# One ring of split weight buffers across four stages of a float32 transformer layer, with expert dots rescheduled and a load moved to another queue

## The reference, cut to what matters

```python
q = (xt @ w_q).reshape(t, PEER_HEADS, 2, PEER_HALF)
sc = jnp.einsum("thpc,hpnc->thpn", q, sub_keys)
top_s, top_i = lax.top_k(sc, PEER_TOPK)
...
best_s, best_pos = lax.top_k(cand_s, PEER_TOPK)
idx = jnp.take_along_axis(cand_i, best_pos, axis=-1)
gate = jax.nn.softmax(best_s, axis=-1)
...
act = jnp.einsum("cd,ced->ce", xc, u[ic])
hid = jax.nn.gelu(act) * gc
return jnp.einsum("ce,ced->cd", hid, v[ic])
```

## Time and profile before

| | |
|---|---|
| median of 3 runs | 2314.18 us (2313.13 to 2315.13) |
| the profiled execution | 2311.03 us, span 2309.1 us |
| TensorE busy | 2165.0 us, 94% of the span |
| TensorE's mean granted clock | 0.968 of 2.4 GHz |
| VectorE, ScalarE, GpSimd busy | 65%, 36%, 29% |
| to 552.5 us | projection, attention, merge, query |
| 552.5 to 1050 us | table |
| 1050 to 1759 us | experts |
| from 1759 us | second layer, output |

### The profile page before, as it was taken

One profiled execution on the slowest core, in us unless ns is written; L12 is line 12 of the kernel. 1 busy time (PEld: TensorE's weight loads), 2 busy tenths in 40 slices (PEclk: granted clock), 3 DMA queues, 4 the chain that ended last, 5 costly groups with the idle time before them and its releaser, 6 DMA issues. The chain is left out here.

```text
span 2309.1 us, 28625 instructions
## 1 busy us (share of the span) xinstructions
PE 2165.0 (94%) x10851; PEld 1874.2 (81%) x10851; DVE 1501.2 (65%) x2669; ACT 826.5 (36%) x1318; POOL 662.4 (29%) x436
## 2 busy tenths in 40 slices
PE   7999899899999978998999999999997999988898
PEld 6777788688999878998788787899986798876677
DVE  4645433325899867864898898869897634447634
ACT  3344423322333324773333333333334332222322
POOL 0100000000117878751444444526661000014200
PEclk9999999999999989999999999999998999988899
DMA  5321533211677766898999999979993322210220
GB/s 209 117 87 47 201 146 124 105 37 51 225 231 211 207 147 149 214 245 292 353 382 388 386 384 375 385 256 381 363 360 122 118 89 95 91 55 1 110 100 37
DMA packets 220089, 454.52 MB, mean 197 GB/s; under 512 B 32305, under 2 KB 137777, under 8 KB 213169
## 3 DMA queue, kind: packets, MB, share of 16 engines
q1 hardware_dynamic: 164656, 318.39, 40.4%
q0 software_dynamic: 55296, 134.31, 17.7%
HBM read 406.17 MB, written 46.47 MB: 196 GB/s over the span
## 5 line engine op out<-in xcount | busy, mean ns | idle before, releaser
L1662 PE MATMUL bank<-Vh,Hh 128*128 128x512 f32 x768 | 302.6, 394 | 14.6 <-DVE Hl L1745 14.6
L1663 PE MATMUL bank<-Vl,Hh 128*128 128x512 f32 x768 | 301.7, 393 | 0.0
L1664 PE MATMUL bank<-Vh,Hl 128*128 128x512 f32 x768 | 301.6, 393 | 0.0
L940 PE MATMUL bank<-XH,Ue 128*128 128x384 f32 x736 | 256.0, 348 | 29.4 <-DVE Ue L929 29.4
L1022 POOL DMA_INDIRECT gates<-rows_sb x128 | 236.4, 1847 | 58.1 <-issue 36.6
L941 PE MATMUL bank<-XL,Ue 128*128 128x384 f32 x736 | 251.4, 342 | 0.0
L942 PE MATMUL bank<-XH,Ue 128*128 128x384 f32 x736 | 251.3, 341 | 0.0
L1684 ACT ACTIVATE Vh<-Vr 128x1024 fp32r<-128x1024 f32 x128 | 135.8, 1061 | 289.0 <-PE bank L1664 181.7
L978 POOL DMA_INDIRECT ring<-in_v,gidx x128 | 187.8, 1467 | 172.2 <-DVE x_res L990 73.6
L978 POOL DMA_INDIRECT ring<-in_u_rows,gidx x98 | 128.8, 1315 | 225.1 <-DVE ghid L983 181.1
L1740 DVE TENSOR_TENSOR Vl<-Vr,Vh 128x1024 fp32r<-128x1024 f32 x128 | 156.3, 1221 | 51.4 <-ACT Vh L1684 51.2
(11 more groups left out here) (394 smaller groups left out, 4845.2 us busy)
## 6 DMA issues: line engine op xcount, KB each, us to landing
Vr<-in_v SPq DMA_DIRECT2D x128, 512.0 KB, 10.1
ur<-in_u SPq DMA_DIRECT2D x86, 512.0 KB, 4.3
W<-in_w_stream SPq DMA_DIRECT2D x19, 2048.0 KB, 8.2
Gr<-gates SPq DMA_DIRECT2D x32, 768.0 KB, 13.9
XT<-in_u SPq DMA_DIRECT2D x42, 512.0 KB, 5.3
early<-ar SPq DMA_DIRECT2D x92, 192.0 KB, 2.3
A<-early SPq DMA_DIRECT2D x92, 192.0 KB, 11.0
xs<-in_w_mixer SPq DMA_DIRECT2D x14, 1024.0 KB, 5.0
```

The source lines that it names most:

```text
L940: pe.matmul(ps, h[:, k], c.Xh[:, k, 0:DN], start=k == 0, stop=False)
L1662: pe.matmul(ps, Hh[r][:, tok], Vh[r][:, cut], start=p == 0, stop=False)
L1663: pe.matmul(ps, Hh[r][:, tok], Vl[r][:, cut], start=False, stop=False)
L1664: mm = pe.matmul(ps, Hl[r][:, tok], Vh[r][:, cut], start=False, stop=p == PK - 1)
```

## The change

The low half of the attention's `kq` tensor now lives from attention to the experts; its upper part holds one ring of two high and two low halves (`c.H`, `c.L`), used by merge, query, table and experts alike. So halves can be made ahead of a border:

- merge piece 0 inside attention, eight units before its end;
- query pieces 0 and 1 inside merge, and query piece 0's product too, behind merge's transposes;
- the table's first two `u` blocks inside query (in place of `hi(16)`, `hi(17)`);
- the experts' first two at the table's end.

The multiplication that makes the fourth tile's input row (`gat.x`) moves from the end of merge into query (after piece 3) and becomes one operation. Blocks per selection and dots per selection change; no fetch is issued between scatter puts. In the experts' stage the gate loads from block 8 on are issued by ScalarE instead of SP, the second gate load comes two steps later, the wait for the stored activations comes after the lead, and `norm_f` is loaded after iteration 8 instead of at the start. Query products use banks 4 to 7 and scores banks 0 to 3.

```diff
-E_SCORE, E_MID, E_SLICES, E_LAST = (14, 19, 19, 19), 0, 8, 5
+E_SCORE, E_MID, E_SLICES, E_LAST = (16, 21, 18, 17), 0, 8, 4
-DOTS = (0, 10, 10, 10)
+DOTS = (0, 12, 4, 0)
...
+    def shared(self, ctx):
+        self.kq = ctx.enter_context(self.nc.sbuf_tensor("kq", [P, LOW + 4 * KT * P], F32))
+        top = self.nc.sbuf_base
+        self.H, self.L = ([self.nc.alloc_sbuf_tensor_at(f"{n}{i}", [P, KT * P], F32R, offset=top - (at - i) * KT * P * 4)[:] for i in range(2)]
+                          for n, at in (("H", 4), ("L", 2)))
...
 # phase_attend, AHEAD = UNITS - 2 * TT
 # VectorE
             for i in range(UNITS + 4):
+                if i == AHEAD + 1:
+                    dve.wait_ge(c.whi, W_MERGE + 1)
+                    dve.tensor_tensor(c.L[0], c.w(B_MERGE, KT * P).rearrange("p k c -> p (k c)"), c.H[0].bitcast(F32), ALU.subtract).then_inc(c.wlo, 1)
 # ScalarE
+                if i == AHEAD:
+                    c.wait_w(act, B_MERGE)
+                    act.activation(c.H[0], c.w(B_MERGE, KT * P).rearrange("p k c -> p (k c)"), ACT.Copy).then_inc(c.whi, 1)
...
 # phase_merge
             transposes_pe(pe, c, mT_rows, T_EXPERTS)
+            ask.products(pe, 0, S_EXPERTS)
...
+            written(act, GP + 2 * OP - 2)
+            ask.hi(act, 0)
             act.wait_ge(c.xlo, S_MERGED + KT)
             norm_sums(act, c, c.X, junk, added, TT)
+            written(act, GP + 2 * OP - 1)
+            ask.hi(act, 1)
             halves_act(act, c, C_G2, T_EXPERTS, Xh)
...
+                if nh == 1:
+                    ask.lo(dve, 0)
...
+            ask.lo(dve, 1)
             halves_dve(dve, c, C_G2, T_EXPERTS, Xh, Xl)
-            dve.wait_ge(c.const_in, CONST_GAIN2)
-            dve.wait_ge(c.scaled, SCALED[T_EXPERTS])
-            dve.tensor_tensor(gat.x[:], mT_rows[:, GT], gat.x[:], ALU.mult).then_inc(gat.rows, 1)
...
+class Asked:
+    def products(self, pe, g, halves=None):
+        c = self.c
+        pe.wait_ge(c.wlo, W_QUERY + g + 1)
+        if g >= 4:
+            pe.wait_ge(self.out_d if g % 2 else self.out_a, g // 2 - 1)
+        h, l, ps = self.half(c.H, g), self.half(c.L, g), self.bank(g)[:]
+        for k in range(KT):
+            if halves is not None:
+                pe.wait_ge(c.xlo, halves + k + 1)
+            pe.matmul(ps, h[:, k], c.Xh[:, k], start=k == 0, stop=False)
+            pe.matmul(ps, h[:, k], c.Xl[:, k], start=False, stop=False)
+            mm = pe.matmul(ps, l[:, k], c.Xh[:, k], start=False, stop=k == KT - 1)
+        mm.then_inc(self.made, 1)
...
 # phase_query, TensorE
-            for g in range(NQ + 1):
+            pe.wait_ge(c.const_in, CONST_KEYS)
+            for g in range(1, NQ + 1):
                 if g < NQ:
+                    ask.products(pe, g)
 # ScalarE (VectorE's lo(g) likewise)
             def hi(g):
                 if g < NQ:
+                    ask.hi(act, g)
+                else:
+                    act.wait_ge(ask.made, g - 1)
+                    early.hi(act, g - NQ)
+
             for g in range(NQ + 2):
-                hi(g + 2)
+                if g < NQ:
+                    hi(g + 2)
 # VectorE
+                    if g == 3:
+                        dve.wait_ge(c.const_in, CONST_GAIN2)
+                        dve.scalar_tensor_tensor(out=gat.x, in0=c.X[:, GT], scalar=c.rn[:, GT:GT + 1], in1=gat.x,
+                                                 op0=ALU.mult, op1=ALU.mult).then_inc(gat.rows, 1)
...
 # phase_table, POOL
-            dots = 0
-            while dots < DOTS[1] + RG:
-                gat.fetch(pool, dots)
-                dots += 1
+            for s in range(DOTS_TABLE):
+                gat.fetch(pool, s)
             for n in range(SCATTERED):
                 pool.wait_ge(chosen, n + 2)
                 for s in range(SLOTS):
-                    if s % BETWEEN == BETWEEN - 1 and dots < DOTS_TABLE:
-                        gat.fetch(pool, dots)
-                        dots += 1
                     sca.put(pool, n, s)
 # VectorE
-            fill(0, EARLY)
+            fill(0, EARLY + 2)
...
 # phase_experts, SP
-                    load_g(0)
-                    load_g(Q_BLK)
-                    for i in range(2):
-                        sp.wait_ge(early.kept[i], 16 * ((EARLY + 1 - i) // 2))
-                    for q in range(LEAD, RA):
-                        load_a(q)
-                    sp.dma_start(nf, t["norm_f"]).then_inc(c.const_in, 16)
+                    load_g(sp, 0)
+                elif m == 3:
+                    load_g(sp, Q_BLK)
+            for i in range(2):
+                sp.wait_ge(early.kept[i], 16 * ((EARLY + 1 - i) // 2))
+            for q in range(LEAD, RA):
+                load_a(q)
             for p in range(PK):
...
                 load_v(p + RR)
-                load_g(p + Q_BLK + 2)
                 load_a(p + RA)
+                if p == RA:
+                    sp.dma_start(nf, t["norm_f"]).then_inc(c.const_in, 16)
 # ScalarE
                 hi_h(p + 1)
+                load_g(act, p + Q_BLK + 2)
                 hi_v(p + 2)
```

More of the change, by code:

```diff
@@ L116 @@
 NTAB = T_PLACE + SCATTERED
+LOW = HEADS // 2 * SEQ
+L_GX = 0
+L_IDX = L_GX + D
+L_GATE = L_IDX + SLOTS
+L_HID = L_GATE + SLOTS
+L_OUT3 = L_HID + SLOTS
+L_GS = L_OUT3 + 3 * P
+L_IOTA16 = L_GS + 2 * PH
 R_GQK = 0
@@ L695, in phase_merge @@
         PIECE = KT * P
-        Wh = [sb(f"Ph{i}", [P, PIECE], F32R) for i in range(2)]
-        Wl = [sb(f"Pl{i}", [P, PIECE], F32R) for i in range(2)]
+        Wh, Wl = c.H, c.L
         zeros = sb("zeros", [P, sca.ZERO])
@@ L717, in piece, with written @@
             return b, c.W[:, b % RING, part * PIECE:(part + 1) * PIECE]
+        def written(act, i):
+            nh, part = divmod(i - GP, OP)
+            act.wait_ge(xg, nh * OG + (OG if part == OP - 1 else part + 1))
         def hi(act, i):
@@ L890, in __init__ @@
         self.raw = [x.rearrange("p (k e) -> p k e", e=P) for x in (c.ur[:, 0], c.ur[:, 1], third)]
-    def buffers(self, ctx, name):
-        made = [ctx.enter_context(self.c.nc.sbuf_tensor(f"{name}{i}", [P, KT, P], F32R)) for i in range(4)]
-        self.Uh, self.Ul = made[0:2], made[2:4]
+        self.Uh, self.Ul = ([x.rearrange("p (k e) -> p k e", e=P) for x in half] for half in (c.H, c.L))
     def table_done(self, eng):
@@ L915, in keep, with hi @@
         sp.dma_start(self.c.t["early"][n], self.c.ar[:, n % 2, 0:DN]).then_inc(self.kept[n % 2], 16)
[L917 to L919 removed]
+    def hi(self, act, n):
+        if n < PK:
             act.wait_ge(self.u_in[n % 3], 16 * (n // 3 + 1))
@@ L982, in dot @@
         dve.wait_ge(self.landed[s % RG], 16 * (s // RG + 1))
-        dve.tensor_tensor_reduce(row, row, self.x[:], 1.0, 0.0, ALU.mult, ALU.add, self.hid[:, s:s + 1]).then_inc(self.used, 1)
+        dve.tensor_tensor_reduce(row, row, self.x, 1.0, 0.0, ALU.mult, ALU.add, self.hid[:, s:s + 1]).then_inc(self.used, 1)
     def add(self, dve, k, to):
@@ L1027, in done, with __init__, piece, half @@
             eng.wait_ge(self.landed[n], 16 * SLOTS)
-def phase_query(c, SC, early):
+class Asked:
+    def __init__(self, c, ctx):
+        self.c = c
+        self.made, self.out_a, self.out_d = signals(c.nc, ctx, "q_grp q_out_a q_out_d")
+    def piece(self, g):
+        return self.c.w(B_PQ + g // 4, KT * 512, 512)[:, :, g % 4 * P:(g % 4 + 1) * P]
+    def half(self, of, g):
+        return of[g % 2].rearrange("p (k e) -> p k e", e=P)
+    def hi(self, act, g):
+        c = self.c
+        c.wait_w(act, B_PQ + g // 4)
+        if g >= 2:
+            act.wait_ge(self.made, g - 1)
+        act.activation(self.half(c.H, g), self.piece(g), ACT.Copy).then_inc(c.whi, 1)
+    def lo(self, dve, g):
+        c = self.c
+        dve.wait_ge(c.whi, W_QUERY + g + 1)
+        dve.tensor_tensor(self.half(c.L, g), self.piece(g), self.half(c.H, g).bitcast(F32), ALU.subtract).then_inc(c.wlo, 1)
+    def bank(self, g):
+        return self.c.bank[4 + g % 4]
+    def products(self, pe, g, halves=None):
+        c = self.c
+        pe.wait_ge(c.wlo, W_QUERY + g + 1)
[9 more added lines that the diff above has]
+        mm.then_inc(self.made, 1)
+def phase_query(c, SC, early, gat, ask):
     nc = c.nc
@@ L1036, in phase_query @@
         sb = lambda name, shape, dt=F32: ctx.enter_context(nc.sbuf_tensor(name, shape, dt))
[L1037 to L1039 removed]
         keys = sb("keys_sb", [P, NQ, PK])
         qT = sb("qT", [P, 2, SEQ])
[L1042 removed]
+        sg, sa, sd = signals(nc, ctx, "s_grp s_out_a s_out_d")
         block = ctx.enter_context(nc.Block())
[L1045 to L1046 removed]
         def query_out(eng, copy, g, sem):
[L1050 to L1051 removed]
+            eng.wait_ge(ask.made, g + 1)
+            copy(qT[:, g % 2], ask.bank(g)[:]).then_inc(sem, 1)
         def scores_out(eng, copy, g, sem):
             eng.wait_ge(sg, g + 1)
[L1056 removed]
+            copy(SC[:, :, g], c.bank[g % 4][:].rearrange("p (t k) -> p t k", k=PK)).then_inc(sem, 1)
         @block.sync
@@ L1088, in _ @@
```

(11 more changed lines are left out.)

116 lines of the change are left out of this document (36 added, 80 removed).

## The result

The changed kernel takes 2323.38 us, the median of 16 runs, beside 2313.65 us for the kernel before on the same chips (16 runs, too). The ratio is 1.0048, with a 95% interval of 1.0034 to 1.0063: slower by half a percent, where 2299.6 us was forecast. It lies outside the range, which ended at 2316.

What follows compares the result with a forecast made beforehand. TensorE was taken as the bound, time being won only where it idles or runs at half clock. Terms summed to -14.6 us, from 2311.03 to 2296.4; with 3.15 for the median, 2299.6 us, range 2276 to 2316.

Steps and rivals of the forecast that it cites:

- Selections and their dots (-30): Table stage: fourth selection no longer waits for gathered rows; 34.3 us lost there, 4 left for exchanges, so -30 us.
- The sign that the prediction named: Fourth selection of the table stage: no VectorE wait for a gathered row, 17 products in about 72 us.
- The scatter's end: Table stage: POOL's 128 puts take some 294 us, 717 to 1011, and hide with 8 us to spare.
- Borders (+0.7 in all up to the table): Stage borders before the table: attention to merge -1, merge to query +1.4, query to table +0.3 us.
- Moved rows (+16): Experts' stage: 14 dots and fetches moved in cost +1.5 at the start, +9.5 in the middle, +5 late.
- norm_f: Experts' stage: its load moved past eight iterations saves 2.3 us at the start, costs 1.4 us in the middle.
- Gates by ScalarE's queue: Experts' stage: same gate bytes issued by ScalarE instead of SP, taken as 0, bounds -6 and +1 us.
- the first rival: Experts' stage: SP's blocked queue, not bytes, holds it; extra rows hide (-17.4), stalls go (-6): 2276 us; chance 0.12.
- The signs given for the experts' stage: Experts' stage some 14 us longer, DMA share at 1.05 with 384 to 390 GB/s.
- The second: Borders give what they could: attention absorbs the split, clock stays up; -6 more, 2293.6 us; chance 0.08.
- the third: Given back: selection gains only 22 us and the experts' late rows cost 11: 2314 us; chance 0.11.
- The fourth rival: Experts' stage: the fetch ring's five buffers decide, extra rows cost 29.4 instead of 17.4 us: 2323 us; chance 0.12.

Runs made afterwards that it cites:

- e3: Kernel before with only the new selection and dot numbers and all 16 fetches ahead of the scatter: 2294.67 us, ratio 0.9926.
- e4: Changed kernel with the wait for the keys moved behind the query stage's second product: 2320.91 us, ratio 1.0025.
- e8: e1 with half the bytes of each gate load from iteration 8 on, other half of the tokens' gates left out: 2264.89 us, ratio 0.9784.
- e10: e6 with the gate table laid out so each partition's twelve 512-byte pieces lie together (6 KB): 2271.94 us, ratio 0.9813.
- e11: e10 with the gate loads issued by ScalarE as in the changed kernel: 2277.42 us, ratio 0.9836.
- e1: Changed kernel with the experts' stage gate loads back in SP's queue, nothing else: 2289.17 us, ratio 0.9901.
- e12: Kernel before with the new gate table layout (long pieces) alone: 2298.24 us, ratio 0.9937.
- e2: Kernel before with only the gate loads from iteration 8 on issued by ScalarE: 2348.44 us, ratio 1.0156.
- e6: Changed kernel with gate loads back on SP and the keys' wait behind the second query product: 2278.6 us, ratio 0.9853.
- e9: e6 with products (15, 20, 19, 18) and dots (0, 11, 5, 0), releasing the scatter two products earlier: 2280.09 us, ratio 0.9844.

## Why the prediction failed

**Selections and their dots (-30): right.** -34.75 after with all borders, of which 0.4 had been put down to the table's last border. TensorE's wait for low halves in the whole table stage fell from 29.4 to 4.0 us, and VectorE waited for a gathered row once, 2.5 us. The sign that the prediction named came as written: the 17 gelus of the fourth selection end 71.7 us after those of the third (790.76 to 862.42), where 72 was said. The 4 us that I had left for exchanges were not needed. The scatter's end was sized too short: 294 us against 298.9 to 310 in the runs without fetches between the puts. In the changed kernel it ended at 1013.1, TensorE's products some 2.5 us later, so it still hid; in e3, e4, e8, e10 and e11 it did not, and in e1 it was late by 0.7 us.

**Borders (+0.7 in all up to the table): right in the sum, by luck in the terms.** The first table product came 0.6 us later than before where the terms sum to 0.7. For attention to merge -0.8 was measured and -1 forecast, but the split cost attention 1.5 us and not 3 (TensorE ended there at 245.58 where it was 244.04; it waits behind the split for 1.24 and 0.51 us, at 232.57 and 234.45), and the 1.7 us for a first stretch at full clock did not come: the granted clock was 0.62 over 244 to 250 and 0.82 over 250 to 256, where it had been 0.76 and 0.96. The keys' wait of 5.07 us came with half clock behind it, and e4 measured their price together at 7.2 us.

**Moved rows (+16): right**, by e3's +16.1. e12 and e10 price them, with the rest of the change, at 709.90 - 693.67 = 16.2 also where the gate pieces are long. **norm_f** wasn't tested by itself: with it and the change's other edits e1's stage stood at +10.9 against before and e3's at +16.1, so by these single profiles they gave 5.2 us, where I had -2.3 + 1.4 = -0.9. Which of them did isn't shown.

**The step that failed** is "Gates by ScalarE's queue ... With the engines full I take 0; bounds -6 (see the first rival) and +1." It measured +34: twice, by e1 and by e2. The step put at nothing a change of queue, because the bytes stay the same. Its bounds came from what the load did to others, as the row of the 8.09 us issue suggested. The other side was missing: what becomes of the load itself. Its row stood in the profile of the kernel before: 13.9 us to landing in SP's queue. In that kernel one load is issued per 16.7 us (15 of them from 1150 to 1400), four iterations ahead of its use, so the reserve was some 3 to 4 us. I had no bound for how late it would land among full engines in another queue, and it needed one: 1536 pieces beside the 4 and 1.5 KB pieces of two other queues. With 27.8 us it was 10 us beyond its date in the worst case, 5.5 in the mean of ten, and TensorE paid, against e1, with 19.8 us of idling and 13.6 us of slower work in the stage. The signs given for the experts' stage show it as well: some 14 us longer at 384 to 390 GB/s was said, 44 us longer at 359 GB/s came; "I am wrong if" named no late gate load.

**The rivals.** The first has the right observation and the wrong value: with the gates gone from SP's queue ScalarE's wait for V did vanish (107.2 to 4.2 us), but no run gained by taking the gates out of that queue. In e1 the wait stood at 152.8 us and the stage was 33 us shorter; with long pieces it was 79.4 us in e10, with the gates in SP's queue, and 106.7 in e11, without them, and the stage was no shorter in e11 (712.91 us against 709.90). The Trainium skill's section that speaks against that rival (DMA: Bandwidth & Descriptors, Issuing engines are not separate DMA queues) held so far; that a second issuer saves only issue time doesn't say that it can cost, and here it cost 34 us. The section that bears on the change itself, on turns between queues, stands on the same page and wasn't weighed. The second and the third did not come either: the borders gave no 6 us more, and the selections gained more than 30 us and not 22. The fourth rival's 2323 us is the number measured, by another mechanism: VectorE waited 3.8 us in the whole run for rows in the ring. A number that comes out right proves nothing of its cause.

**Left open.** Why the 128 puts take 299 us in one kernel and 310 in another. What one turn of a DMA engine moves, and why about every second load is the late one. A third gate buffer, which might let ScalarE's loads be early enough, wasn't tried.

## What to carry to other kernels

When a load moves to another queue, ask first when it will land there and not only what it frees behind it: here the loads took up to 17 us standing in line in SP's queue and up to 27.8 in one of their own, where the other two queues got three to four times the bytes; with long pieces the same move cost little or nothing. Before sizing an edit against a DMA share of 1, divide the share by queue and by bytes: a queue that takes 15% of the engines for 12% of the bytes is a layout to mend, and mending it here (15.8 us) was worth nearly as much as the rescheduling alone (18.9 us, by e3). And a gain ahead of a long parallel chain, here POOL's scatter, is checked against that chain's end, with its measured length and not its least.

## What was not expected of the hardware

- A load of 768 KB in 512-byte pieces took 7.5 to 17.0 us to land (13.9 in the median) in a queue shared with the other loads. In a queue of its own ten of 30 took 21.0 to 27.8 us. The engines were full in both.
- Pieces of 512 bytes took 45% more engine time per byte than pieces of 6 KB (1.43% against 0.98% of 250 us of 16 engines for each MB), and with long ones the rate of the whole rose to 399 GB/s from 357 in the changed kernel, and to 395 from 384 in the kernel before.
- The same 128 scatter puts took between 299 and 310 us; between e6 and e9 (299 and 305) most of the difference lies in gaps that the profile calls issue.
